# Row items by tile, logits turned first and gates made late in the routing stage of a two-layer decoder step with experts

## What is computed

```python
def hier_moe(h, w_r1, b_r1, w_r2, b_r2, w_gate, w_up, w_down):
    ...
    g_prob = jax.nn.softmax((xt @ w_r1).astype(F32) + b_r1, axis=-1)
    p_grp, grp = lax.top_k(g_prob, 1)
    e_all = jnp.einsum('nd,gde->nge', xt, w_r2).astype(F32) + b_r2
    e_logit = jnp.take_along_axis(e_all, grp[:, :, None], axis=1)[:, 0]
    p_e, e_idx = lax.top_k(jax.nn.softmax(e_logit, axis=-1), TOP_IN_GROUP)
    p_e = p_e / jnp.sum(p_e, -1, keepdims=True)
    expert = grp * EXPERTS_PER_GROUP + e_idx
    gate = jnp.zeros((n, N_EXPERTS), F32).at[jnp.arange(n)[:, None], expert].add(p_grp * p_e)
    hid = jax.nn.silu(jnp.einsum('nd,edf->nef', xt, w_gate)) * jnp.einsum('nd,edf->nef', xt, w_up)
    y = jnp.einsum('nef,efd->nd', hid * gate[:, :, None].astype(hid.dtype), w_down)
```

## Time and profile before

| | |
|---|---|
| median of 3 runs | 2512.09 us (2508.17 to 2515.15) |
| the profiled execution's own time | 2504.79 us |
| its span | 2503.2 us |
| busy: PE, PEld, DVE, ACT | 94%, 58%, 26%, 20% of the span |
| mean granted clock of TensorE | 0.967 |

### The profile page before, as it was taken

The page is one execution under the profiler, slowest core; times in us unless marked ns, Lnnn a source line. Parts: engine busy times, 40 slices in busy tenths (PEclk is TensorE's granted clock), DMA queues, the critical chain, the costliest instruction groups (busy, mean ns, idle before and its releaser), DMA issues.

```text
span 2503.2 us, 32244 instructions
## 1 busy us (share of the span) xinstructions
PE 2341.8 (94%) x12521; PEld 1443.3 (58%) x12521; DVE 663.3 (26%) x1245; ACT 501.5 (20%) x1125; POOL 4.2 (0%) x10
## 2 busy tenths in 40 slices
PE   6999999989999999898989998999999999999997
PEld 4768786678643434343568876645786343434345
DVE  0159911601551121212210000022025412121213
ACT  1120106510320101010210014633004200101014
POOL 0000000000000000000000000000000000000000
PEclk9999999989899999999989999999899999999999
DMA  8624457783149898989635446998440699989890
GB/s 272 188 78 158 145 168 232 224 304 135 68 178 428 341 429 346 429 360 429 247 107 163 147 153 212 358 338 288 173 164 34 281 391 380 424 359 429 363 392 35
DMA packets 210136, 647.70 MB, mean 259 GB/s; under 512 B 56841, under 2 KB 90266, under 8 KB 184154
## 3 DMA queue, kind: packets, MB, share of 16 engines
q1 hardware_dynamic: 174650, 636.31, 65.8%
q10 hardware_dynamic: 35376, 9.91, 1.7%
HBM read 640.19 MB, written 5.96 MB: 258 GB/s over the span
## 4 chain that ended last, share of the span: by engine, by line
PE 74%; DMA 13%; SPq 4%; ACT 3%; DVE 2%; ACTq 2%; issue 2%; DVEq 0%
PE bank L606 17%; PE bank L1180 11%; PE bank L1029 9%; PE bank L1165 8%; PE bank L1210 7%; DMA ring<-in_w_down 6%; DMA ring<-in_w_up 5%; PE bank L1224 5%; PE bank L784 3%; SPq L389 3%; ACTq L389 1%; PE bank L793 1%; ACT arena L1295 1%; PE bank L924 1%; PE bank L1085 1%
## 5 line engine op out<-in xcount | busy, mean ns | idle before, releaser
L1180 PE MATMUL bank<-ring,AT 128*64 128x512 f32 x2048 | 451.2, 599 | 27.6 <-DMA ring<-in_w_up 25.8
L1295 ACT ACTIVATE arena<-bank 128x512 f32<-128x512 f32 (+3 forms) x523 | 258.0, 542 | 946.8 <-PE bank L606 414.7
L606 PE MATMUL bank<-X,ring 128*128 128x264 f32 x1664 | 373.8, 388 | 1.2 <-ACT arena L1295 1.2
L606 PEld LDWEIGHTS bank<-X,ring 128*128 128x128 f32 x1664 | 317.8, 191 | 56.1 <-ACT arena L1295 1.4
L1180 PEld LDWEIGHTS bank<-ring,AT 128*64 128x64 f32 x2048 | 147.0, 138 | 323.0 <-issue 287.6
L1210 PE MATMUL bank<-ring,arena 128*64 128x512 f32 x1024 | 233.3, 612 | 32.7 <-DMA ring<-in_w_down 23.7
L1029 PE MATMUL bank<-AT,ring 128*128 128x264 f32 x1024 | 239.1, 397 | 7.1 <-DVEq L1861 7.1
L1029 PEld LDWEIGHTS bank<-AT,ring 128*128 128x128 f32 x1024 | 200.6, 196 | 43.7 <-issue 7.9
L2092 DVE TENSOR_TENSOR X<-bank,X 128x264 f32<-128x264 f32 x256 | 110.7, 433 | 395.3 <-PE bank L1224 392.4
L1165 PE MATMUL bank<-arena 128*128 128x256 bf16 (+1 forms) x1440 | 191.1, 273 | 0.5 <-DVE arena L1947 0.5
L1210 PEld LDWEIGHTS bank<-ring,arena 128*64 128x64 f32 x1024 | 77.0, 140 | 178.7 <-issue 155.6
(11 more groups left out here) (304 smaller groups left out, 1458.9 us busy)
## 6 DMA issues: line engine op xcount, KB each, us to landing
ring<-in_w_gate SPq DMA_DIRECT2D x64, 2048.0 KB, 17.1
ring<-in_w_up SPq DMA_DIRECT2D x64, 2048.0 KB, 13.0
ring<-in_w_down SPq DMA_DIRECT2D x64, 2048.0 KB, 16.7
ring<-in_w_o SPq DMA_DIRECT2D x16, 2048.0 KB, 10.4
ring<-in_cache_b_k SPq DMA_DIRECT2D x128, 256.0 KB, 4.2
ring<-in_cache_b_v SPq DMA_DIRECT2D x128, 256.0 KB, 4.9
ring<-in_w_in_a SPq DMA_DIRECT2D x14, 2048.0 KB, 9.1
ring<-in_w_in_b SPq DMA_DIRECT2D x12, 2048.0 KB, 8.3
```

Of the source, the lines that this page charges most:

```text
L606: mm = pe.matmul(B[4 * (g % 2) + f][:, 0:n_tok], u[:, c * 512 + f * P:c * 512 + (f + 1) * P], src[8 * half + c][:, 0:n_tok], start=(half = ...
L1180: mm = pe.matmul(B[bank][64 * s:64 * s + 64, :], M.xsT[:, at:at + 64], ring[slots[s][0]][:, c * FE:(c + 1) * FE], start=(half == 0 and c = ...
L1295: return act.activation(out, in_, ACT.Copy, scale=scale)
```

## The change

- **Row items by tile.** Item n is now token tile n//4 and quarter n%4: items 0 to 3 are the four quarters of the first 128 tokens, 4 to 7 those of the second. Their four corrections use operands at partitions 0, 32, 64 and 96, and are issued one behind the other (items 0 to 3, then 4 to 7, then 8 and 9).
- **Seven banks.** Items use banks 4, 5, 6, 0, 1, 2, 3, 4, 5, 6 rather than four in turn, so only items 7 to 9 wait for a bank. The idle products write bank 0.
- **Logits turned first.** Only item 0 is turned ahead of the logits, items 1 to 3 after them.
- **Ranks moved up.** On PE the ranks stand directly behind the raw rows of items 4 and 5; the corrections of 4 to 7 and all of items 6 to 9 come behind. The four idle products ahead of the ranks are gone; six stand ahead of the gather, after a wait for four rests.
- **Gates behind the parts.** `route` finds the second expert on shifted logits, not on their exponentials, so up to `chosen` it waits for no exponential. The sums, reciprocals and weights move to `gates`, behind the last low part. ACT's first router exponential stands behind two high parts, the second (now 128 x 3) behind middle part 1.
- DVE makes two pairs of low and rest ahead of the slots where it made three.

The first piece is PE's order in the routing stage of before, from the last logits product (L1122) to the rows of item 6 (L1085 is `raw_rows`, L1097 `fix_rows`, L1053 the idle products, L1143 the ranks).

```diff
@@ -59,7 +59,7 @@
 N_ITEMS = 10
-ROW_BANKS = [4, 5, 6, 0]
+ROW_BANKS = [4, 5, 6, 0, 1, 2, 3, 4, 5, 6]
 ITEMS = [("self", t, hp, P * (t + 1)) for t in range(2) for hp in range(6)] + \
...
@@ -391,7 +391,7 @@
             if n < 8:
-                q, t = divmod(n, 2)
+                t, q = divmod(n, 4)
                 g, h = divmod(q, 2)
...
@@ -1076,10 +1076,10 @@
                 q, t, _ = row_item(n)
-                bank = B[ROW_BANKS[n % 4]]
+                bank = B[ROW_BANKS[n]]
                 pe.wait_ge(S("ln_scaled"), KC * layer + (4 * q + 4 if t < 2 else KC))
-                if n >= 4:
-                    pe.wait_ge(S("rest_made"), N_ITEMS * layer + n - 3)
+                if n >= 7:
+                    pe.wait_ge(S("rest_made"), N_ITEMS * layer + n - 6)
                 for c in range(4):
...
@@ -1106,8 +1106,7 @@
-                for n in range(4):
-                    raw_rows(layer, n)
+                raw_rows(layer, 0)
                 pe.wait_ge(S("logits_copied"), layer + 1)
...
@@ -1122,15 +1121,15 @@
                 mm.then_inc(S("router_rows"), 1)
+                for n in range(1, 4):
+                    raw_rows(layer, n)
                 pe.wait_ge(S("fix_ready"), layer + 1)
                 pe.wait_ge(S("gain_rows"), 32 * (layer + 1))
                 for n in range(4):
                     fix_rows(layer, n)
                 for n in range(4, 6):
                     raw_rows(layer, n)
-                    fix_rows(layer, n)
-
-                idle_products(4)
+
                 pe.wait_ge(S("chosen"), layer + 1)
...
@@ -1142,10 +1141,16 @@
                 mm.then_inc(S("ranks"), 1)
-                for n in range(6, N_ITEMS):
+                for n in range(6, 8):
                     raw_rows(layer, n)
+                for n in range(4, 8):
                     fix_rows(layer, n)
-                idle_products(4)
+                for n in range(8, N_ITEMS):
+                    raw_rows(layer, n)
+                for n in range(8, N_ITEMS):
+                    fix_rows(layer, n)
+                pe.wait_ge(S("rest_made"), N_ITEMS * layer + 4)
+                idle_products(6)
                 pe.wait_ge(S("low_made"), N_ITEMS * (layer + 1))
...
@@ -1561,17 +1566,19 @@
                     act.wait_ge(S("r_shifted"), 2 * layer + k + 1)
-                    act.activation(M.a4[8 + k], M.a4[k], ACT.Exp).then_inc(S("r_exp"), 1)
+                    shifted = (M.a4[0], M.c1[3])[k]
+                    act.activation((M.a4[8], M.c1[9])[k], shifted, ACT.Exp).then_inc(S("r_exp"), 1)
                 act.wait_ge(S("row_scale"), layer + 1)
-                router_exp(0)
                 row_high(layer, 0)
                 row_high(layer, 1)
-                router_exp(1)
+                router_exp(0)
                 for n in range(2, N_ITEMS + 2):
                     if n < N_ITEMS:
                         row_high(layer, n)
                     row_mid(layer, n - 2)
+                    if n == 3:
+                        router_exp(1)
                 def gather_copies(done):
...
@@ -1975,37 +1982,26 @@
                 first_of(og)
-                sel, gate, slot, t16 = M.w16
+                sel, slot, t16 = M.w16[0], M.w16[2], M.w16[3]
                 link(dve.tensor_tensor(v4(t16), lg[:, :, 4:20].rearrange("p t (g e) -> p t g e", g=4), by_group(og), ALU.mult))
                 link(dve.tensor_reduce(el, t16.rearrange("p (t g e) -> p t e g", t=3, g=4), AX.X, ALU.add))
                 link(dve.tensor_reduce(mx, el, AX.X, ALU.max))
-                dve.tensor_tensor(ep, el, b3(mx, 4), ALU.subtract).then_inc(S("r_shifted"), 1)
-                dve.wait_ge(S("r_shifted"), 2 * layer + 2)
+                link(dve.tensor_tensor(ep, el, b3(mx, 4), ALU.subtract))
                 rests(layer, range(2))
                 link(dve.scalar_tensor_tensor(t4, ep, 0.0, first, ALU.is_equal, ALU.mult))
                 first_of(o1)
-                dve.wait_ge(S("r_exp"), 2 * layer + 2)
-                link(dve.tensor_reduce(sm_, ge, AX.X, ALU.add))
-                link(dve.reciprocal(pg, sm_))
-                link(dve.scalar_tensor_tensor(ee, o1, -2.0, ee, ALU.mult, ALU.add))
-                link(dve.tensor_reduce(v2, ee, AX.X, ALU.max))
-                link(dve.tensor_tensor(t4, ee, b3(v2, 4), ALU.is_equal))
+                link(dve.scalar_tensor_tensor(ep, o1, NEG, ep, ALU.mult, ALU.add))
+                dve.tensor_reduce(v2, ep, AX.X, ALU.max).then_inc(S("r_shifted"), 1)
+                dve.wait_ge(S("r_shifted"), 2 * layer + 2)
+                link(dve.tensor_tensor(t4, ep, b3(v2, 4), ALU.is_equal))
                 link(dve.tensor_tensor(t4, t4, first, ALU.mult))
                 first_of(o2)
-                link(dve.tensor_scalar(den, v2, 1.0, None, ALU.add))
-                link(dve.reciprocal(den, den))
-                link(dve.tensor_tensor(w1, den, pg, ALU.mult))
-                link(dve.tensor_tensor(w2, v2, w1, ALU.mult))
-                link(dve.tensor_tensor(tmp, o1, b3(w1, 4), ALU.mult))
-                link(dve.tensor_tensor(t4, o2, b3(w2, 4), ALU.mult))
-                link(dve.tensor_tensor(tmp, tmp, t4, ALU.add))
-                link(dve.tensor_tensor(o1, o1, o2, ALU.add))
-                link(dve.tensor_tensor(o1, o1, b3(cst("valid"), 4), ALU.mult))
-                link(dve.tensor_tensor(v4(sel), by_expert(o1), by_group(og), ALU.mult))
-                link(dve.tensor_tensor(v4(gate), by_expert(tmp), by_group(og), ALU.mult))
+                link(dve.tensor_tensor(both, o1, o2, ALU.add))
+                link(dve.tensor_tensor(both, both, b3(cst("valid"), 4), ALU.mult))
+                link(dve.tensor_tensor(v4(sel), by_expert(both), by_group(og), ALU.mult))
                 dve.sem_inc(S("chosen"), 1)
-                for n in range(3):
+                for n in range(2):
                     lows(layer, [n])
...
@@ -2013,6 +2009,26 @@
                 link(dve.tensor_copy(M.cnt, B[7][:, 48:64]))
+
+            def gates(layer):
+
+                v3 = lambda x, n: x.rearrange("p (t k) -> p t k", k=n)
+                b3 = lambda x, n: x.unsqueeze(2).broadcast_to((P, 3, n))
+                og, t4, o1, o2, tmp, ge = [v3(M.a4[k], 4) for k in (2, 3, 4, 5, 6, 8)]
+                sum_, pg, w1, w2, den, e2 = [M.c1[k] for k in (1, 2, 4, 5, 6, 9)]
+                gate = M.w16[1].rearrange("p (t g e) -> p t g e", t=3, g=4)
+                dve.wait_ge(S("r_exp"), 2 * layer + 2)
+                link(dve.tensor_reduce(sum_, ge, AX.X, ALU.add))
+                link(dve.reciprocal(pg, sum_))
+                link(dve.tensor_scalar(den, e2, 1.0, None, ALU.add))
+                link(dve.reciprocal(den, den))
+                link(dve.tensor_tensor(w1, den, pg, ALU.mult))
+                link(dve.tensor_tensor(w2, e2, w1, ALU.mult))
+                link(dve.tensor_tensor(tmp, o1, b3(w1, 4), ALU.mult))
+                link(dve.tensor_tensor(t4, o2, b3(w2, 4), ALU.mult))
+                link(dve.tensor_tensor(tmp, tmp, t4, ALU.add))
+                link(dve.tensor_tensor(gate, tmp.unsqueeze(2).broadcast_to((P, 3, 4, 4)),
+                                       og.unsqueeze(3).broadcast_to((P, 3, 4, 4)), ALU.mult))
...
@@ -2107,14 +2123,15 @@
                 link(dve.tensor_copy(d3, v3(slot, 16)[:, :, 0:4]), 0)
-                link(dve.tensor_copy(g3, v3(gate, 16)[:, :, 0:4]), 0)
                 link(dve.tensor_tensor(sel12, cst("slot").unsqueeze(1).broadcast_to((P, 12, CAP)),
                                        M.d3.unsqueeze(2).broadcast_to((P, 12, CAP)), ALU.is_equal), 0)
                 dve.tensor_copy(bump, M.no[:, 1:2]).then_inc(sm("chosen_slots"), 1)
-                for n in range(3, N_ITEMS):
+                for n in range(2, N_ITEMS):
                     lows(layer, [n])
                     if n + 2 < N_ITEMS:
                         rests(layer, [n + 2])
+                gates(layer)
+                link(dve.tensor_copy(g3, v3(gate, 16)[:, :, 0:4]), 0)
                 link(dve.tensor_tensor(sg12, sel12, M.g3.unsqueeze(2).broadcast_to((P, 12, CAP)), ALU.mult), 0)
```

More of the change, by code:

```diff
@@ L1052, in idle_products @@
                 for _ in range(n):
-                    pe.matmul(B[3][:, :], cst("ones"), consts[:, 0:512], start=True, stop=True)
+                    pe.matmul(B[0][:, :], cst("ones"), consts[:, 0:512], start=True, stop=True)
             def router_weights(layer):
@@ L1549, in row_high @@
                 act.wait_ge(S("token_rows"), N_ITEMS * layer + n + 1)
-                src = B[ROW_BANKS[n % 4]][:, :].rearrange("r (p j) -> r j p", j=8)
+                src = B[ROW_BANKS[n]][:, :].rearrange("r (p j) -> r j p", j=8)
                 act.activation(out[0], src, ACT.Copy, scale=M.c1[8][:, t:t + 1]).then_inc(S("high_made"), 1)
@@ L1960, in route @@
                 lg = v3(M.lg, 20)
-                gp, ep, og, t4, o1, o2, tmp, el, ge, ee = [v3(x, 4) for x in M.a4]
-                mx, sm_, pg, v2, w1, w2, den, f1 = M.c1[0:8]
```

(2 more changed lines are left out.)

## The result

The changed kernel takes 2486.6 us (median of 4 runs, 2484.7 to 2489.0) against 2510.1 before (2506.9 to 2515.2): 23.6 us faster, ratio 0.9905, 95% interval 0.9884 to 0.9926. The prediction was 2499.1, 13 us faster, with a range of 2489 to 2509.

What follows compares the result with a forecast made beforehand. The loop over experts is bound by transfers and begins only when the gather ends. Earlier gathers save 8.8 and 5.4 us, together 14.2, less 0.6 a layer: 13.0; 2512.1 - 13.0 = 2499.1 us, range 2489 to 2509.

Steps and rivals of the forecast that it cites:

- A microsecond of the stage is one of the kernel: Routing stage: each microsecond by which the gather starts earlier saves one microsecond of the whole kernel, once in each layer.
- Logits first, 2.8 us for DVE and 0.9 kept: Stage's start: three items of turning leave the logits' way; DVE starts 2.8 us earlier, only 0.9 us is kept.
- Gates late: Ahead of `chosen`: DVE makes 12 instructions, not 22; the gates' 2.3 us behind the last low part cost nothing.
- Four corrections in 1.1 us: PE in the routing stage: corrections of four different quarters overlap and take 1.1 us together, against 2.02 before.
- The tail: Stage's end: from item 4's high part, 1.3 us, then 9.0 us of low parts and rests to the gather.
- The clock: Routing stage: clock falls in both layers, ranks and items 6 and 7 at half; 14.2 us saved, not 22.3.
- The 0.6 us a layer charged for the gather's clock: Gather's start: PE stands some 2 us ahead of it, so a piece runs at half clock, 0.6 us a layer.
- The forecast's own case: Routing stage: clock falls and is back by the second corrections or soon after; 9 to 18 us saved, 52%.
- PE's longer stop: PE ahead of the ranks: a stop of 2.8 us, against 1.65 before, behind light work; clock expected to fall.
- The clock did not stay at full: Rival for the routing stage: the clock stays at full, 22.3 us saved, span 2480.9 or 2489.8 us; 15%.
- The low clock up to the idle products: Rival for the routing stage: PE's ranks, turns and corrections all at half clock, 6.8 us saved, 2505.3 us; 20%.
- The slower rival: Rival for the gather: half clock throughout in both layers costs 38 us, result 2536 us; 5%.

Runs made afterwards that it cites:

- the two neighbours: Two versions of the changed kernel: old pairwise item numbering (median 2485.4 us), and three idle products added in PE's stop ahead of the ranks (median 2486.1 us).
- v_fix_first: Changed kernel with turns of items 6 and 7 and corrections of 4 to 7 ahead of the ranks, nine idle products ahead of the gather: median 2487.1 us.
- u_pairs: Changed kernel with the old item numbering, so four corrections fall into two row groups instead of four: median 2485.4 us.

## Why the prediction was wrong, step by step

- **A microsecond of the stage is one of the kernel.** Right for what the stages gave, wrong for the whole. This step failed, and it is about half of the error of 10.6 us. The forecast took everything behind the start of the gather as fixed ("a microsecond by which it starts earlier is a microsecond of the whole kernel"), so the loops stood in the sum at nothing. They have the same work, but not the same clock: they gave 5.1 us (4.2 with the two neighbours). In v_fix_first they took back 6.3.
- **Logits first, 2.8 us for DVE and 0.9 kept.** The reciprocal came 2.7 us earlier and `sel` at 10.7 us, 10.6 forecast. What the undone version lost was 5.5 us in layer 0 and 2.0 in layer 1, for light work stood side by side again and the clock was down for 23.9 and 6.8 us, not 3.4. The step's mechanism is right, its worth was not in it.
- **Gates late.** The ten instructions were 2.07 us of PE's stop in the version that undoes them, as worked out. The forecast missed what else this buys: with the gates early the ranks ran at half clock, and one gather too. The gates behind the parts were hidden, as said: from gather to `gate_up` it is 20.0 and 20.1 us, as before.
- **Four corrections in 1.1 us.** They took 1.14. This is worth nothing on the path (u_pairs), as ACT takes a bank in 0.7 us. The trace agrees with the estimate of 1.1 us that the prediction drew from the Trainium skill (TensorE: Matmul & The Clock Gate, Part 3).
- **The tail.** 10.3 us from item 4's high part to the gather was forecast; 680.20 to 690.54 is 10.3.
- **The clock.** This step failed too, in the words "ranks and items 6 and 7 at the half". The clock fell once in each stage, but behind the ranks and not ahead of them: they took 2.48 us, not 4.7, and the corrections began 17.0 us behind the first turn, not 19.0. That is 2 us a layer. The 0.6 us a layer charged for the gather's clock did not occur. 13.0 + 4.0 + 1.2 is 18.2, and 18.5 was measured in the stages. The forecast's own case does exist: layer 1 without the idle products had its fall ahead of the ranks and its corrections at 19.0 us, as forecast, but none of the four profiles with the changed kernel's stage did. The reason given for the fall, PE's longer stop, was not borne out: with the stop filled the clock fell just the same. The rows of before already spoke against it. The forecast reads the first fall as one "around a stop of 1.65 us" and the second as "behind the turns of 8 columns"; but the first came at 663.8, while PE was still in the corrections and just ahead of the stop (663.92 to 665.57), and the second at 687.6, when the turns at 687.50 had just begun (windows of the kernel before):

```profile
663.85:664.00 0.15, 0.07 (x2) 0.00 (x0) 0.12 (x2) 0.15 (x2) 0.00 (x0) 0.50 0.00 0
687.70:688.00 0.30, 0.30 (x6) 0.18 (x4) 0.30 (x1) 0.30 (x1) 0.00 (x0) 0.50 0.00 0
```

- **The rivals.** The clock did not stay at full (22.3 us was its price, near the total by chance of other terms). The low clock up to the idle products did not come. The slower rival did not come in this kernel, but its mechanism is real in two neighbours. Its price was put at 19 us a gather and measured as 13.7, 15.2 and 7.2.

Still open is what sets the place of a fall, in the stage and inside the loops. The runs show that the falls in the loops change when the start of the loop moves, and that the fall 80 us in costs 1.7 us on the 16 products behind it; they do not show what sets a loop's whole length.

## What to carry to other kernels

On PE, try an order of light products (few rows, few columns) and dense ones in which two light stretches do not meet, and price a move by what it does to the granted clock, not only by what it frees: here one move was worth nothing in one order and 7.5 us of the stages in another. Measure a kernel without its filler products before taking them out: six that seem to cost time, ahead of a long dense stretch, protected 14 us a layer by the medians. Where the clock falls differs between executions of the same code, so profile a version more than once. And after shortening a stage, check that the untouched stages kept their length before believing or dismissing the total.

## What the runs showed that was not expected

- 144 gather products without a gap kept the half clock for 34.3 us in layer 0 of the version without idle products, and for 16 us in its layer 1. Idle products of 512 columns had it back inside their 5.59 us in the kernel before.
- The same nine rank products (18 records) take 2.4 to 2.5 us at full clock and 3.9 to 4.4 at or near the half, so light products too pay nearly double.
- A correction of 2 rows alone takes 1.12 us, four of quarters 0, 0, 1, 1 took 2.02, and four of quarters 0 to 3 took 1.14: in the traces their records start in pairs in the one order and four together in the other.
